# Four chunks of gathered expert rows between the last pre-products of the dense experts

## The reference, cut to what matters

```
qry = (xt @ w_query).reshape(PEER_BLOCK, PEER_HEADS, 2, PEER_KEY_DIM)
s1, s2 = qry[:, :, 0] . keys1, qry[:, :, 1] . keys2     # 128 keys each
v1, i1 = top_k(s1, 16);  v2, i2 = top_k(s2, 16)
top_s, pos = top_k(v1[..., :, None] + v2[..., None, :], 16)
gate = softmax(top_s)
act = gelu(einsum('td,thkd->thk', xt, expert_u[idx]))
out = einsum('thk,thkd->td', gate * act, expert_v[idx])
```

## Time and profile before

| | |
|---|---|
| runs | 4268.82, 4273.96, 4277.01 us (median 4273.96) |
| span of the profiled execution, first to last instruction | 4268.7 us |
| time of the profiled execution with what lies around the span | the profile gives the span alone; the median of the runs is 5.3 us above it |
| PE / DVE / POOL / ACT busy | 88% / 61% / 44% / 19% |
| mean granted clock of TensorE | 0.936 |
| bytes moved by DMA | 1063.93 MB, 249 GB/s over the span |

### The profile page before, as it was taken

The page is one execution under the profiler, slowest core; times in us unless marked ns, Lnnn a source line. Parts: engine busy times, 40 slices in busy tenths (PEclk is TensorE's granted clock), DMA queues, the critical chain, the costliest instruction groups (busy, mean ns, idle before and its releaser), DMA issues. The chain is left out here.

```text
span 4268.7 us, 42974 instructions
## 1 busy us (share of the span) xinstructions
PE 3771.0 (88%) x15498; PEld 2781.4 (65%) x15498; DVE 2617.9 (61%) x5356; ACT 810.4 (19%) x1637; POOL 1894.6 (44%) x1714
## 2 busy tenths in 40 slices
PE   8889998978999999993598899999789999999934
PEld 7646787867766666642485477887676666666424
DVE  4765216645677667687658652166456676667875
ACT  2243302224000000000222522022330000000011
POOL 6102004764455555566370020057645555555663
PEclk9899999989999999996798999999899999999967
DMA  3201234558999999999622102345579999999996
GB/s 102 109 30 40 69 138 117 128 155 273 383 405 409 409 397 409 387 409 361 255 81 109 37 33 85 138 120 119 158 271 401 406 409 409 398 409 386 409 355 250
DMA packets 333955, 1063.93 MB, mean 249 GB/s; under 512 B 79152, under 2 KB 96176, under 8 KB 312496
## 3 DMA queue, kind: packets, MB, share of 16 engines
q0 software_dynamic: 184320, 537.08, 34.5%
q1 hardware_dynamic: 132368, 505.22, 31.4%
q10 hardware_dynamic: 17056, 18.88, 1.3%
HBM read 1025.27 MB, written 35.78 MB: 249 GB/s over the span
## 5 line engine op out<-in xcount | busy, mean ns | idle before, releaser
L1648 PE MATMUL bank<-v_tile,shared 128*128 128x512 f32 x2048 | 910.2, 599 | 38.2 <-DVE shared L2009 35.6
L2059 POOL DMA_INDIRECT u_rows<-in_peer_u,idx_all x512 | 653.7, 1277 | 641.5 <-DVE act_u L1967 519.0
L1979 DVE SCALAR_TENSOR_TENSOR x<-v_rows,act_w,x 128x1024 f32<-128x1024 f32 x512 | 657.8, 1285 | 260.0 <-DMA v_rows<-in_peer_v,idx_all 234.8
L2059 POOL DMA_INDIRECT v_rows<-in_peer_v,idx_all x512 | 589.3, 1151 | 415.5 <-DVE x L1979 304.2
L1648 PEld LDWEIGHTS bank<-v_tile,shared 128*128 128x128 f32 x2048 | 392.9, 192 | 494.2 <-issue 447.3
L1967 DVE CUSTOM_DVE_ANT_0 u_rows<-u_rows,h 128x1024 f32<-128x1024 f32 x512 | 606.6, 1223 | 121.3 <-DMA u_rows<-in_peer_u,idx_all 120.4
L2069 POOL DMA_INDIRECT first_cells<-first_gate,cell_all x256 | 415.3, 1622 | 579.1 <-DVEq L1959 466.8
L1636 PE MATMUL bank<-hT,bT 128*128 128x256 f32 x2048 | 453.9, 380 | 0.0
L1636 PEld LDWEIGHTS bank<-hT,bT 128*128 128x128 f32 x2048 | 389.9, 191 | 74.3 <-issue 23.9
L1540 PE MATMUL bank<-hT,ring 128*128 128x256 f32 x1536 | 341.1, 383 | 14.2 <-PEq L150 14.2
L1540 PEld LDWEIGHTS bank<-hT,ring 128*128 128x128 f32 x1536 | 293.6, 192 | 56.5 <-issue 15.8
(11 more groups left out here) (367 smaller groups left out, 5013.5 us busy)
## 6 DMA issues: line engine op xcount, KB each, us to landing
v_tile<-in_peer_v SPq DMA_DIRECT2D x256, 512.0 KB, 7.4
ring<-in_w_in_panels SPq DMA_DIRECT2D x76, 1024.0 KB, 4.9
bT<-in_peer_ut SPq DMA_DIRECT2D x128, 512.0 KB, 7.6
ring<-in_peer_w_query SPq DMA_DIRECT2D x32, 1024.0 KB, 5.2
aT<-in_peer_ut SPq DMA_DIRECT2D x64, 512.0 KB, 6.8
sT<-in_peer_ut SPq DMA_DIRECT2D x64, 512.0 KB, 6.9
ring<-in_ple_w_gate SPq DMA_DIRECT2D x24, 1024.0 KB, 8.1
first_cells<-zeros SPq DMA_DIRECT2D x16, 1024.0 KB, 11.5
```

Source lines behind the costliest of these rows:

```text
L1648: ins = mm(acc[t][part][:, :], act_pair[p % AHEAD][:, at:at + P], v_tile[:, e % DENSE, part * 512:part * 512 + 512], start=(e == 0), stop= ...
L1979: stt(out=m.x[:, 2 + t, :], in0=vr[:, n % RINGS, :], scalar=act_w[:, p % 4, i:i + 1], in1=m.x[:, 2 + t, :], op0=ALU.mult, op1=ALU.add).the ...
L2059: nc.gpsimd.indirect_dma_start(out=rows[:, n % RINGS, :], out_offset=None, in_=table, in_offset=bass.IndirectOffsetOnAxis(ap=idx_all[:, t, ...
```

## The change

The six steps `pre` 6 to 11 now have the chunks 4, 5, 6 and 7 among them: one behind the first, third, fourth and sixth of the six. The loop over the remaining chunks begins at chunk 8 and spreads the 64 pairs over 48 chunks up to chunk 56, not over 52. No instruction is added or taken away. POOL's own order stays as it was.

```
@@ -1333,6 +1333,7 @@
 OCT_PAIRS = OCT // 2
 QUADS = P // 4
 HOT_CHUNKS = 4
+CHUNKS_BESIDE = (0, 2, 3, 5)
 CELLS = P * KEYS * P
 CELL_OCT = OCT * P
 LATE_CHUNKS = 4
@@ -1386,11 +1387,15 @@
             order.append(("pre", pairs))
             pairs += 1
     order.append(("hot", QUADS))
+    begun = HOT_CHUNKS
     for p in range(pairs, AHEAD):
         order.append(("pre", p))
+        if p - pairs in CHUNKS_BESIDE:
+            order += chunk(begun)
+            begun += 1
     done = 0
-    for c in range(HOT_CHUNKS, CHUNKS + 2):
-        goal = min(PAIRS_ALL, -(-(c - HOT_CHUNKS + 1) * PAIRS_ALL // (DENSE_END - HOT_CHUNKS)))
+    for c in range(begun, CHUNKS + 2):
+        goal = min(PAIRS_ALL, -(-(c - begun + 1) * PAIRS_ALL // (DENSE_END - begun)))
         for p in range(done, goal):
             if p + AHEAD <= PAIRS_ALL:
                 order.append(("pre", p + AHEAD))
```

## The result

The changed kernel is slower: 4286.43 us (4277.53 to 4290.54, 13 runs) against 4270.37 us for the kernel before in the same rounds, a ratio of 1.0033 with a 95% interval of 1.0027 to 1.0040. That is 14 us by the ratio and 16 between the medians, where 4267.4, some 7 us faster, had been forecast. Its profiled execution took 4285.5 us, 4283.7 of them from the first to the last instruction.

A forecast was written before the change was run, and what follows sets the result against it. The stage was taken as some 700 us at PE's pace, then some 250 us at the gathers'. Per layer +11 + 3 - 10 - 7, more exactly -3.3, for two layers -6.6, gave 4267.4 us, range 4248 to 4290.

The forecast's parts named there:

- Step 1: Chunks 4 to 7 run where DVE waited for gates; they delay the first gating and PE's first `values`: +11 us a layer.
- slower rival: PE waits for gates behind the chunks on DVE's queue: start 27 us late, 4299 us in all; chance 0.20.
- Step 2: PE's waits inside the row of `pre`, behind ACT's gelus: the cover of two banks holds, 0 us.
- Step 3: PE's clock falls after a wait at the first `values`: about +3 us once, nothing without a wait.
- Steps 4 and 5: Behind the pairs: one chunk more done by `values` 50, -10.3 us; DVE's larger lead at the handover, -7 us a layer.
- lead at pair 50: Gating of pair 52 to PE's product of pair 50: stays 15.0 us or reaches 28.7; half taken, -7 us.
- decisive point: Delay of PE's first `values` from which the slower rival decides against the change: some 15 us.
- rule of turns between queues: DMA engines alternate between gather and load queues: 20.5 us a chunk, a delay of about 32 us; price not taken.
- The second count: Bound on the gain: idle DMA share of the hole, 45% of 27 us, 12 us a layer; extreme 4250.

The follow-up runs named there:

- h1: Changed kernel with the `peer_ut` loads for groups 14 to 27 cut to a quarter of their columns, 5.5 MB less per layer: 4260.37 us.
- f1: Changed kernel with three chunks in place of four, behind the first, fourth and sixth of the six `pre` steps: 4277.33 us.
- e1: Changed kernel with three chunks (4, 5, 6) in the row of pre-products, not four: 4273.67 us.
- g5: Changed kernel with two chunks in place of four, behind the first and fourth step, `DENSE_END` 56 as before: 4265.88 us.
- e3: Changed kernel with the fourth chunk, chunk 7, moved right behind the first `values` step and its gating: 4294.59 us.
- e5: Changed kernel with the gathers of rows 20 to 31 (chunks 5, 6, 7) on 32 of 128 partitions only: 4269.26 us.
- g2: Kernel before the change with `DENSE_END` 58 in place of 56, no chunk in the hole: 4246.87 us.
- g4: Changed kernel with two chunks in place of four, behind the first and fourth step, and `DENSE_END` 58: 4214.71 us.

## Why the forecast was wrong, step by step

**Step 1, the chunks in the hole, is the step that failed.** It had +11 us for PE, and the first gating at 1099.3, and its own sign of being wrong was a first product after 1106. Measured: 18.7 us, the gating at 1107.4 and the product at 1108.3. The mechanism was as put down (a gating behind 16 additions on DVE's queue), and its size was wrong. The four chunks took 68.3 us (1039.1 to 1107.4), not 60.5. The whole difference is waiting for gathers: DVE waited 27.6 us for them in the four chunks, and 19.7 us in the stretch from 1084.5 to 1148.4 from which I took the length. Two steps of mine can be read off the rows:

- I took 3.5 us off for the gatings, as if DVE set the pace of that stretch. It didn't, as the 19.7 us of waiting show; in the hole the time without gatings was filled by waiting.
- I took the start of the stretch for that of the hole. In the stretch POOL issues the first gather for chunk 5 1.5 us after chunk 4 begins, and DVE's wait for it is 0.7 us. In the hole it comes 7.8 us after (1046.88 against 1039.10), behind the last four scatters, while the last store of the dense gates moves 2.1 MB, and DVE waits 5.4 us. My slower rival had named both and put them aside as over by 1053.

The loads of `gates` and `v_tile` look like a third, but they are not the missing bytes: the loads of SP moved 10.3 MB in the 68.3 us of the hole and 12.7 MB in the 63.9 us of the stretch. No run takes the scatters or the store out of the hole, so how much each of them costs stays open. That bytes count there is shown by h1: 14.6 us for 5.5 MB.

The profile had the evidence for too much work, too: the window from 1053 to 1080 was 55% busy, so 12 us of DMA were free in it, against 41 us that four chunks need. I used that number only for a bound on the gain, not for a bound on how much fits without delay. Two chunks delay PE by 3 us, three by 6 to 7, four by 19.

**Step 2, no waits of PE inside the row of `pre`, failed by 3 us.** The moved scores cost 0.9 us there (they cost the same later before the change, so this is a shift), and ACT's gelu behind chunk 6 cost 2.1. In the changed kernel this costs nothing more, since PE waits 15.2 us for DVE behind it. f1 showed that removing the wait brings nothing as long as `v_tile` is late too. That load, which PE waits for in e1, f1 and g5, was in none of my steps.

**Step 3, the clock, was right in kind.** The forecast said 3 us; the first product took 8.9 instead of 7.0 us, and by pair 52 the stretch had cost 1.0 us more than before (750.2 against 749.2). The rule of the Trainium skill that the forecast cited from "TensorE: Matmul & The Clock Gate", section "HAM oscillation — how this bites in real kernels" (the next burst after a wait for data starts cold), agrees with the 8.9 us.

**Steps 4 and 5, what comes back behind the pairs, were near in sum.** The forecast was 10.3 + 7; measured 14.7 and 15.7 in the two layers. The lead at pair 50 is 21.6 us, half way between 15.0 and the most, as these two rows of the changed kernel show (gating of pair 52, product of pair 50, which answer to the earlier trace rows):

```profile
1816.24 0.42 DVE L2011 TENSOR_TENSOR shared<-shared,gates 128x256 f32<-128x256 f32 x1
...
1837.79 2.74 PE L1653 MATMUL bank<-v_tile,shared 128*128 128x512 f32 x6
```

That it came out so is luck. Half was a choice, and the lead swings from pair to pair with the place of the chunks in the list: at pair 44 it is 10.7 us where it was 28.7, and e3, e5 and h1, which have nearly the same list, show the same 21.6 and 10.7. e1 has 8.5 at pair 50 and still 9 us less behind V52 than before. So the lead at one pair was no measure of what comes back.

**The sum.** With the measured sizes, 18.7 + 1.0 - 14.7 = +5.0 us a layer, where -3.3 had been forecast; 7.7 of these 8.3 us are step 1. The decisive point lies near where the slower rival had put it, at a delay of some 14 us. That rival, PE waiting for the gates behind the chunks, is what happened, at 19 us and not at 27. Its price one to one was right (h1 against the changed kernel: 12.5 us at V0, 12.8 at the end). The rule of turns between queues of the Trainium skill ("DMA: Bandwidth & Descriptors", section "Queues, rings and completion order"), which I had priced at 32 us, is further from the 18.7 than my own 11. No run here shows the turns themselves; from 1053 to 1080 the gathers had 67% of the engines and the loads 35%, not half each.

**The second count** (all that can be won is the idle share of the hole, 12 us a layer) held for the end at 56, where the best kernel won 5 and 4. It is no bound once the end moves. g2 wins 14 and 12 us a layer without touching the hole, from DMA time that was idle elsewhere: 384 GB/s became 406 in the 97 us ahead of pair 52, and 363 became 370 behind it. And g4 wins 16 and 13 us a layer on top of g2. I hadn't asked what `DENSE_END` does.

**What stays open.** Of the 14 to 16 us between the medians, about 10 are shown in the stage. The rest agrees in size with the clock in the attention of layer 1, but I have one profiled execution of the changed kernel, so its share in the median is not shown. That two and three chunks at 58 leave the same 238 us behind V52 fits the 49 chunks that both have begun there, and the same lead of 21.7 us at pair 50.

## What to carry to other kernels

Before work is moved into a hole, take the hole's free share of the resource that the work needs (here 12 us of DMA) and compare it with the work's need (10 us a chunk); the idle time of the engine that runs it (DVE, 44 us) says little. Then ask where the work goes on that was behind it: if a fixed end spreads the rest thinner, as here, the bytes won in the hole are idle time later, and little or nothing of them is kept. When a moved step stands in an in-order queue ahead of something that the pacing engine needs, its lateness passes on one to one, and the number that decides is how many chunks, so try one or two next to the number that fills the hole. Try also the end of the stretch that the change thins: here moving it by two chunks was worth 24 us and two chunks in the hole 5, and the two together 56, or 1.3%.

When a length is taken from another place of the same kernel, compare how the two begin, and don't take off the time of an engine that is waiting there.

## What the runs showed of the hardware that I had not expected

- Gathers on 32 of 128 partitions kept the DMA engines full: share 1.05 at 266 GB/s, where whole ones have 1.03 at 411. The unchanged 512 KB loads of `peer_ut` beside them took 10.4 to 10.9 us to land, where it was 6.7 to 7.4. So a share of 1.0 does not tell that the DMA moves all it can.
- From issue to landing a 512 KB gather took 17.5 and 21.5 us on the chain of the changed kernel in the full DMA.
- The same code at the same place ran at a granted clock of 0.91 in some programs, of 0.50 in others and of 0.72 in one, for 18 us. The way from the chunks of layer 0 to those of layer 1 was 5 to 9 us longer in those with 0.50.
